# Twenty products of zeros behind the last back products of three expert loops

## What is computed

```python
def hierarchical_moe(h, w_group, b_group, w_expert, b_expert, w_gate, w_up, w_down):
    g_idx = jnp.argmax(g_prob, axis=-1)                # one group per token
    top_w, top_i = lax.top_k(e_prob, TOP_K)            # two experts in it
    combine = jnp.sum(jax.nn.one_hot(expert_id, N_EXPERTS) * weights[..., None], axis=1)
    gate = jnp.einsum('td,edf->tef', xb, w_gate)
    up = jnp.einsum('td,edf->tef', xb, w_up)
    act = jax.nn.silu(gate) * up * cb[..., None]
    return jnp.einsum('tef,efd->td', act, w_down)

for i in range(DEPTH):                                 # twice, in two blocks of two layers
    h = rms_norm(x, norm1_g[i])
    x = x + mixer(h) @ w_out
    x = x + hierarchical_moe(rms_norm(x, norm2_g[i]), ...)
```

## Time and profile before

| | |
|---|---|
| median of three runs | 1649.4 us (1646.24 to 1652.56) |
| the profiled execution | 1649.91 us, its span 1648.2 us |
| mean granted TensorE clock | 0.963 |
| TensorE products (PE) | 1477.3 us busy, 90% of the span |
| TensorE weight loads (PEld) | 819.9 us, 50% |
| VectorE (DVE) | 743.1 us, 45% |
| ScalarE (ACT) | 492.0 us, 30% |
| GpSimd (POOL) | 97.9 us, 6% |
| DMA | 467.31 MB, mean 284 GB/s |

### The profile page before, as it was taken

How to read it: one execution, slowest core, us unless ns; L and a number is a source line. 1 busy time by engine, 2 the same in 40 slices (tenths; PEclk the granted TensorE clock), 3 DMA queues, 4 the chain that set the end, 5 groups by cost and what they waited for, 6 DMA issues and landing times. The chain is left out here.

```text
span 1648.2 us, 23801 instructions
## 1 busy us (share of the span) xinstructions
PE 1477.3 (90%) x9307; PEld 819.9 (50%) x9314; DVE 743.1 (45%) x1578; ACT 492.0 (30%) x967; POOL 97.9 (6%) x238
## 2 busy tenths in 40 slices
PE   8999899888699998988869988998989969899995
PEld 4586533222375653322227776776563337656332
DVE  1656522222435544221237745665762246677322
ACT  3221211101216311110126555655231135641211
POOL 0000011100000001110001001000001000000110
PEclk9999999999799999999989999999989989998998
DMA  9976489999753185999996450435368993618795
GB/s 371 370 313 240 194 351 420 420 420 421 324 228 149 56 369 225 420 421 421 421 424 239 153 211 20 153 143 190 120 266 347 420 409 129 230 59 326 289 420 238
DMA packets 62111, 467.31 MB, mean 284 GB/s; under 512 B 7664, under 2 KB 15776, under 8 KB 17184
## 3 DMA queue, kind: packets, MB, share of 16 engines
q1 hardware_dynamic: 61984, 465.59, 69.8%
HBM read 462.81 MB, written 2.76 MB: 282 GB/s over the span
## 5 line engine op out<-in xcount | busy, mean ns | idle before, releaser
L1547 PE MATMUL PS<-ring,catT 128*32 128x512 f32 x3072 | 355.8, 606 | 38.8 <-issue 27.6
L793 PE MATMUL PS<-w_split,h_split 128*128 128x512 f32 x1152 | 274.6, 396 | 10.1 <-DVE w_split L878 10.1
L793 PEld LDWEIGHTS PS<-w_split,h_split 128*128 128x128 f32 x1152 | 213.8, 189 | 64.6 <-DVE w_split L878 17.0
L1547 PEld LDWEIGHTS PS<-ring,catT 128*32 128x32 f32 x3072 | 101.8, 111 | 261.4 <-issue 261.4
L1570 PE MATMUL PS<-ring,hidden_cols 128*32 128x512 f32 x1472 | 167.0, 593 | 30.0 <-issue 26.3
L878 DVE TENSOR_TENSOR w_split<-ring,w_split 128x512 fp32r<-128x512 f32 x192 | 132.4, 710 | 74.8 <-ACT w_split L826 74.2
L826 ACT CAST w_split<-ring 128x512 fp32r<-128x512 f32 x192 | 118.0, 619 | 112.8 <-PE PS L793 112.2
L1839 DVE SCALAR_TENSOR_TENSOR xn_split<-PS,slot_w,xn_split 128x512 fp32r<-128x512 f32 x96 | 71.7, 751 | 160.9 <-ACT xn_split L1683 160.7
L1692 ACT ACTIVATE hidden_rows<-PS 128x256 f32<-128x256 f32 x48 | 18.4, 383 | 409.6 <-PE PS L1547 409.6
L1570 PEld LDWEIGHTS PS<-ring,hidden_cols 128*32 128x32 f32 x1472 | 50.2, 109 | 140.6 <-issue 140.5
L1683 ACT ACTIVATE xn_split<-PS,slot_w 128x512 fp32r<-128x512 f32 x96 | 65.5, 687 | 156.4 <-PE PS L1570 135.0
(11 more groups left out here) (409 smaller groups left out, 1679.0 us busy)
## 6 DMA issues: line engine op xcount, KB each, us to landing
ring<-in_moe SPq DMA_DIRECT2D x284, 1024.0 KB, 18.7
ring<-in_w_ada SPq DMA_DIRECT2D x16, 3072.0 KB, 11.3
ring<-in_a_w_in SPq DMA_DIRECT2D x23, 2048.0 KB, 12.2
ring<-in_b_w_in SPq DMA_DIRECT2D x8, 2048.0 KB, 22.7
ring<-in_a_w_out SPq DMA_DIRECT2D x2, 3072.0 KB, 10.7
ring<-in_b_w_out SPq DMA_DIRECT2D x2, 3072.0 KB, 9.8
ring<-in_w_mem_kv SPq DMA_DIRECT2D x2, 2048.0 KB, 11.3
first_down<-in_moe SPq DMA_DIRECT2D x4, 1024.0 KB, 11.2
```

Of the source, the lines that this page charges most:

```text
L793: last = nc.tensor.matmul(PS[:, 2 * (i % 2) + t, :], hs[:, hp, k, t * P:(t + 1) * P], wk[:, (KT * i + k) % splits, wp, :], start=k == 0 an ...
L1547: last = nc.tensor.matmul(PS[lanes, 4 + i % 2, :].rearrange("p (g f) -> p g f", g=2), xf[:, i % 2, k, lanes], gate_up_weights(2 * i + q % ...
```

## The change

Behind the `If` and the `Else` branch of `moe`, in TensorE's program alone, twenty products of zeros into bank 4 are added where another layer follows, that is for m = 0, 1 and 2.

```diff
@@ -1638,6 +1638,8 @@
                         nc.tensor.sem_inc(down_ready.sem, 2 * NP)
                         nc.tensor.sem_inc(combined.sem, NP)
                         nc.tensor.sem_inc(y_ready.sem, 1)
+                    if then == "norm":
+                        keep_busy(4, 20)
 
                 @block.scalar
                 def _(act):
```

## The result

The changed kernel takes 1666.9 us (median of four runs, 1664.27 to 1670.68) against 1648.2 us for the kernel before beside it (1646.24 to 1652.56). The ratio is 1.0102, with a 95% interval of 1.0082 to 1.0122: slower, by 13.5 to 20 us. The profiled execution took 1666.23 us, 16.3 us more than the one before. So the direction was forecast rightly. The forecast of 1662 is 4.9 us too low, inside its range of 1655 to 1668.

What follows compares the result with a forecast made beforehand. TensorE was taken to have no instruction until its 6.1 to 6.5 us jump ends, so the products delay the barrier. +2.95 (A), +5.65 (B) and +4.05 (C) make +12.65 us on 1649.91, forecast 1662 us, range 1655 to 1668.

Steps and rivals of the forecast that it cites:

- the first rival: At the jumps, products run inside the idle gap and all gains are kept: 5.4 us faster, 1644 us; 6 in 100.
- The second rival: At all three places, zeros do not raise the clock and nothing comes back: +25 us, 1674 us; 5 in 100.
- A: Expert loop 0 into the latent attention, about 429 us: 6.55 us later, 3.6 back, net +2.95 us.
- B: Expert loop 1 into the dilated attention, 855 us: 6.55 us later, 0.9 back, net +5.65 us.
- The third rival: In the expert loops behind the places, a DMA-bound loop absorbs the delay: about 1651 us; 5 in 100.
- The length of twenty products: Behind each jump, twenty products take 4.31 us at full clock, longer at half clock: 6.3 us forecast.
- T: Time of the twenty products behind each jump: 4.31 + s / 2, put at 6.3 us, ends 4.3 and 7.7.
- s: Part of the products' stretch behind each jump run at half clock, taken as 4.0 us.
- What comes back: Behind the products, transposes and following work run at full clock: 3.6 us back at A, 0.9 at B and C.
- C: Expert loop 2 into the forgetting attention, 1344 us: 6.55 us later, 1.6 slack and 0.9 back, net +4.05 us.
- The slack of 1.6 us at C: At the barrier behind expert loop 2, TensorE arrives 1.6 us before VectorE, which hides that much of the delay.

Runs made afterwards that it cites:

- The first experiment: The changed kernel with its twenty products of zeros moved into the If branch, ahead of the jump: 1652.5 us, ratio 1.0035 to the kernel before.
- the last kernel: Products ahead of the jump and 64 unexecuted zeros in loop 1's Else branch, plus nine zeros before the last back products: 1644.2 us, ratio 0.997.

## Why the prediction was right, and where its sizes were off

**The products start behind the jump: right, and shown.** The prediction read from the earlier trace rows that TensorE has nothing to issue for 6.1 to 6.5 us. In the trace after the first load of zeros comes 0.06 us after the jump's end, within the 0.2 us named. With the jump cut to 0.33 us the delay fell from 22.1 to 0.4 us, and with the products ahead of the jump they ran at once. That also closes the first rival (1644 us): in this code nothing is issued before the jump has landed, since its code is still being fetched (the packet in the jump, above).

**Zeros raise the clock: right.** The second rival (1674 us) would have had 0.43 us for each of the twenty. At A they took 5.8 us in all, at B 7.4, and the transposes behind them 1.94 us at all three places. The prediction says that no product of zeros had met the low clock in the trace of before. That was misread: three of the 117 did, from 1222.4 on (the longest took 634 ns), and the clock rose at 1223.6, during the third.

```profile
L359 PE MATMUL PS<-zero x117: 376/379/634, 187.9 to 1521.6; 128*128 128x512 bf16 x117
```

**Nothing absorbs the delay: right.** The third rival (1651 us) falls. The expert loops behind the places took 223.0, 107.7 and 107.7 us and now take 221.8, 107.4 and 107.8: 1.3 us less in all.

**The length of twenty products: the rule right, its input wrong.** T = 4.31 + s / 2, with 0.17 us for the last one, gives 5.8 us for the s = 2.7 us read at A and 7.4 us for s = 5.9 us at B. That is what the rows have: 436.00 to 441.81, and 862.87 to 870.27. The prediction took s = 4.0 everywhere. At A this was 0.7 us too much, at B 0.9 us too little; that the two nearly cancel (net 9.2 us at A and B together, 8.6 forecast) is luck. Why the clock comes up after 2.7 us in one place and after 5.9 us in another no run was made to find out.

**What comes back: right at A, a little too much at B and C.** Forecast were 3.6, 0.9 and 0.9 us, measured 3.6, 0.6 and 0.6. At A most of it is the work of L2541 that had run at half clock, as the prediction had it. At B and C the products L793 follow the first transpose after 3.25 us, where 3.84 - 0.9 = 2.9 was forecast. VectorE's L891 came 1.1 us after it, as forecast, but the way from there to L793 took 2.15 us at B and not the same 1.86: VectorE's L878 now waited 0.32 us for ScalarE's L826.

**The step that failed is the sum at C.** T was put at 6.3 us, with the last product's 0.17 us 6.5. The products took 1367.80 - 1357.35 = 10.45 us. Without the break it would have been 4.31 + 2.95 / 2 + 0.17 = 5.95, and the kernel with its code moved by 128 instructions has 6.03 there. The break adds 3.03 - 0.22 = 2.8 us from the start of one product to the start of the next, and the clock that fell behind it, from 1363.7 to 1367.1, another 1.7 us. Together that is 10.45. This term alone is 4.0 us too small, most of the difference between the 12.65 us of the forecast and the 17.4 of the account. The slack of 1.6 us at C was taken off rightly: 10.45 + 0.05 - 1.6 = 8.9, against 8.8 measured.

The break is shown to be a matter of where the code lies, by the two kernels that moved it, and the packets of queue 8 show what it waits for: the same fetch of instructions as the long jump. At the four places with a break one packet ends 1.4 to 1.5 us before the jump does. The next starts 3.2 to 3.5 us after the landing, and the code beyond the edge goes on 1.3 to 1.5 us after the end of this second packet, that is 5.7 to 6.0 us after the landing. What sets the 3.2 to 3.5 us no run here shows. The Trainium skill, Runtime: NRT & Kernel Launch, section Instruction fetch mechanics, says that instructions are fetched in blocks of 256, one sequential block ahead, and that the cost of crossing a block's end is "mostly hidden". The trace agrees with the block, 16,384 bytes in a packet, and with the place of its edge, which eight more instructions moved by eight. It differs on the cost right behind a jump: 0.47 to 3.82 us were not hidden. The prediction had cited this section for the jump and had not asked what it means for the code behind the landing.

**The first experiment's expectation failed** by what it left out: the moved code brought such a break to B. The 0.8 us that twenty products ahead of the jump take to issue, at A and B, where the barrier waits for the jump behind them, lie within the 2 us it had allowed. With the break taken away the ratio went from 1.0035 to 0.9979. That is 9 us, and the expectation was 3 to 5; the profiled executions of the two kernels are 3.5 us apart, and where the rest comes from is not shown.

## What to carry to other kernels

Idle time of an engine in a profile is not always time in which it could work: look at its sequencer's records first, and put filler ahead of a long jump, never behind it. Filler in front of a barrier is paid for in full unless it ends before the last of the others arrives; twenty products cost 22.1 us behind three long jumps and 0.4 us behind short ones. After any edit that moves code behind a long branch, look for a break in the first few microseconds after its landing; it can move or vanish by instructions that are never executed.

## What the hardware showed that was not expected

- A second break follows the landing of a long jump when the code there soon passes the edge of a 16,384-byte block: 0.47, 2.65 and 3.82 us in products of zeros, 3.49 us ahead of a transpose. It ends 5.7 to 6.0 us after the jump's end, 1.3 to 1.5 us after a DMA packet of instructions, and its place moves with the code, instruction by instruction.
- The jump's length does not grow with the number of experts jumped over: 5.8 to 7.8 us at A and B (32 experts) and at C (16), in all kernels run here that have the unrolled loop. Behind the last layer, also over 16, it took 3.4 to 5.4 us. Without the loop it took 0.33, 0.19 and 0.30 us at A, B and C.
- Issuing twenty products of zeros and their weight loads held the sequencer for some 0.8 us in the first experiment, though they ran for 5.6 us, and for 0.4 us in the last kernel, at full clock.
- The granted clock rose from half to full 2.7, 5.9 and 2.95 us after the first zero at A, B and C of one execution, and fell again 3.4 us after its rise at C, behind the 2.65 us break.
